# The residual stream of a two-layer trunk kept by rows between layers, with another order of the output projection and another split of the weight ring

## The chip, the core and the metric

One core of a Trainium2 chip. The metric is the device time of one execution of the whole kernel in microseconds, median of the runs. Its parts that matter here: TensorE (PE, matmuls and transposes through PSUM banks), VectorE (DVE), ScalarE (ACT), GpSimd (POOL), SyncE (SP, which issues all transfers). Each engine works through its own list of instructions in order and waits on semaphores.

## The reference, cut

Two layers over x of 512 rows (tokens) by 1024 columns, then a last norm, all in float32:

```
h = rmsnorm(x, norm_w)                  # rows of 1024
proj = h @ w_in                         # 1024 x 4160: 33 column tiles
y = concat(rwkv7(...), short_conv(...), moba_attention(...), retention(...)) * silu gates
x = x + y @ w_out                       # 1024 x 1024
...                                     # after both layers: out = rmsnorm(x, final_norm_w)
```

## The kernel before, in words

**Layout.** The stream x stands turned: `XY` holds 8 tiles of 128 model columns (partitions) by 512 tokens. The split copy of h, `act_hi` and `act_lo`, has the same layout. Every float32 product is made of three (high x high, low weight x high, high weight x low); `product(job, n)` issues the three for one of 8 blocks of the contraction, and a job is 8 such blocks, 24 matmuls of 512 columns (16 for `wa`).

**Norm.** At the start x is loaded by rows (4 tiles of 128 rows), turned by 32 transposes into `XY` and also spilled to scratch memory, since `XY` is used again for the gated outputs y. The sum of squares of the first layer is taken on the rows; rms is broadcast over the partitions by four small matmuls (`norm`), VectorE scales (`scaled`), ScalarE rounds to the high part, VectorE makes the low part (`low`), and TensorE starts the pair `k0`, `k1` tile by tile. Between layers the squares are added up by VectorE and summed over partitions by small matmuls (`stat`). After the last layer each output tile is turned back to rows by four transposes (`row`), multiplied by the final norm's weight, and at the very end scaled by 1/rms and stored.

**Weights.** The stream of a layer is 33 tiles of `w_in` (numbers 0 to 32: k0, k1, wa, r0, r1, v0, v1, rwkv_g0, rwkv_g1, rq0, rq1, rk0, rk1, rv0, rv1, ret_g0, ret_g1, mq0, mq1, mk0, mk1, mv0, mv1, moba_g0, moba_g1, cc0, ...) and 8 of `w_out`. SyncE loads tile i into one of `RAW` buffers when tile i - `RAW` is split. The high part goes to one of `HI` buffers when the job `HI` places earlier is through; it is made on ScalarE in `weight_high(job)`, called right behind each job's own evacuation, for tile number job + `HI`, or on GpSimd for the tiles in `POOL_HIGH`. GpSimd makes all low parts. ScalarE's list behind `weight_high` goes on with the evacuations of the next steps.

**Order.** `layer_steps()` writes one list of steps; each engine issues its part of every step in that order. Around tile 20 it reads: gate ret_g1; `to_rows("rk")` (8 transposes, two evacuations by ScalarE); `block_rows(2)` (VectorE, the end of the 16x16 block inverses); quarters 0 and 1 of mq0; `retain_state` on TensorE, which waits for those evacuations; and on. SyncE's list has, in front of the load of tile 18 (mq1), the copies of the score blocks out and back (`blocks_out`), and in front of the load of tile 20 (mk1):

```
def inverses_back(layer):
    sp.wait_ge(*at("blocks_done", layer))       # VectorE, block_rows(2)
    ...                                         # blocks out to scratch, then 8 loads back
if j == TILES.index("mk1"):
    inverses_back(layer)
load_weights(i)
```

**Output projection.** `project_out(m)`: eight jobs of 24 matmuls, weights stationary, y moving; the first two interleaved block by block as y gets split (`split_y`). VectorE adds each to the x tile that has come back from scratch (L1776).

Of the kernel before, what the change touches and what calls it, by code (L numbers as in the profile page):

```python
# [50 lines left out]
RAW, HI, LO = 3, 3, 3  # L51
# [18 lines left out]
OUT_TILES = [f"out{m}" for m in range(KT)]  # L70
STREAM = TILES + OUT_TILES

POOL_HIGH = ("mk1", "mv0", "mv1", "moba_g0")
# [11 lines left out]
MU, W0, A0, KKP, KAP, RKP, LNW, LNB, CONVW, NORMW = 0, 7, 9, 11, 13, 15, 17, 19, 21, 27  # L85
N_ROWS, N_PAR = 27, 35
# [6 lines left out]
CONSTS = [("ident", 128), ("eps", 2), ("one", 1), ("head_mean", 128), ("all_mean", 1), ("causal", 128),  # L93
# [44 lines left out]
def layer_steps():  # L138

    s = [("norm",), ("k_pair",)]  # L140
# [51 lines left out]
    s += [("conv_out", 1)] + [("split_y", k) for k in Y_ORDER[5:]] + [("project_out", m) for m in range(KT)]  # L192
# [15 lines left out]

Y_ORDER = [6, 7, 4, 5, 0, 1, 2, 3]
STEPS = layer_steps()  # L210


def bank_jobs():


    pro = [("norm_cols", 7, 1)] + [(f"x_in{m}", m, 1) for m in range(KT)] + [("params0", 3, 1), ("params1", 4, 1)]
# [3 lines left out]
    def proj(name, readers):  # L220
        if name not in projections:

            at = {"wa": 2, "out0": 0, "out1": 4}.get(name)
            if at is None:
                at = (int(name[3:]) + 1) % 2 if name.startswith("out") else (len(projections) - (len(projections) > 2)) % 2
            layer.append((name, at, readers))
            projections.append(name)
# [7 lines left out]
    for step in STEPS:  # L235
        kind = step[0]
        if kind == "norm":
            layer.append(("rn", 2, 0))
        elif kind == "k_pair":
# [55 lines left out]
        elif kind == "retain_values":  # L295
            layer.append((f"ret_y{step[1]}", 4, 1))
        elif kind == "retain_state":
            layer.append(("ret_state", 4, 1))
        elif kind == "ln_var":
            layer += [("var0", 7, 1), ("var1", 5, 1)]  # L300
        elif kind == "ret_stat":
            layer += [("ret_ms0", 2, 1), ("ret_ms1", 3, 1)]
        elif kind == "project_out":
            proj(f"out{step[1]}", 1)
            if step[1] == KT - 1:
                layer.append(("stat", 2, 1))
    epi = [(f"row{m}", 3 + m % 5, 1) for m in range(KT)]
    return pro, layer, epi


def trunk_kernel(nc, x, norm_w, w_in, w_out, rwkv_mu, rwkv_w0, rwkv_w2, rwkv_a0, rwkv_a2, rwkv_k_k,
                 rwkv_k_a, rwkv_r_k, rwkv_lnx_w, rwkv_lnx_b, conv_w, rel_bias, final_norm_w,
                 consts, level_masks, ret_eps, x_scratch, bias_scratch, a_scratch, t_scratch, tt_scratch, out):
    pro, per_layer, epi = bank_jobs()
    place = {}
    full_count, read_count = [0] * 8, [0] * 8
    for part, names in (("pro", pro), ("layer", per_layer), ("epi", epi)):
        if part == "layer":
            pro_full, pro_read = list(full_count), list(read_count)
            full_count, read_count = [0] * 8, [0] * 8  # L320
        if part == "epi":
            lay_full, lay_read = list(full_count), list(read_count)
            full_count, read_count = [0] * 8, [0] * 8
        for name, bank, readers in names:
            place[part, name] = (bank, full_count[bank], read_count[bank], readers)
            full_count[bank] += 1
            read_count[bank] += readers

    def locate(name, layer):


        part = "pro" if layer < 0 else "epi" if layer >= DEPTH else "layer"
# [6 lines left out]
    with ExitStack() as ctx:  # L339
# [16 lines left out]
        par = sb("params", [P, DEPTH, N_PAR])  # L356
        der = sb("params_derived", [P, DEPTH, N_DER])
        lora_w = sb("lora_w", [2 * LORA, DEPTH, G])
        small = sb("small", [P, 32])
# [19 lines left out]
        ident, head_mean, all_mean = const("ident"), const("head_mean"), const("all_mean")  # L379
# [19 lines left out]
        out_rows = pages[:, 17 * PG:(17 + NT) * PG].rearrange("p (t c) -> p t c", c=PG)  # L399
        norm_rows = page(10)[0:DEPTH * KT, 0:P]  # L400
# [6 lines left out]
        fnorm = page(2)  # L407
        row_sum, row_scale, row_max = small[:, 0:4], small[:, 4:8], small[:, 20:24]
        mean_sq, root, rms = small[:, 8:12], small[:, 12:16], small[:, 16:20]
        UW = pages[:, 21 * PG:21 * PG + 2048].rearrange("p (m x i) -> p m x i", m=MATS, x=2)  # L410
# [10 lines left out]
        def s(name):  # L421
# [9 lines left out]
            "h_raw": KT, "h_hi": KT, "h_split": KT,  # L431
# [29 lines left out]

        block = ctx.enter_context(nc.Block())
# [3 lines left out]
        def _(sp):  # L466
# [5 lines left out]
            load(norm_rows, norm_w.rearrange("l (k c) -> (l k) c", c=P), "norm_loaded")  # L472
# [3 lines left out]
            def load_weights(i):  # L476

                layer, j = divmod(i, n_stream)
                if i >= RAW:
                    sp.wait_ge(s("w_split"), i - RAW + 1)  # L480
                n = 2 * LORA if STREAM[j] == "wa" else P
                if j < len(TILES):
                    c = TILE_COLS[TILES[j]]
                    src = w_in[layer, :, c:c + n]
                else:
                    src = w_out[layer, :, (j - len(TILES)) * P:(j - len(TILES) + 1) * P]
                sp.dma_start(w_raw[:, i % RAW, :, 0:n], src.rearrange("(k p) c -> p k c", p=P)).then_inc(s(f"w_loaded{i % RAW}"), 16)
# [19 lines left out]
            load_weights(2)  # L507
# [45 lines left out]
            def spill_first_x():  # L553
                for m in range(KT):
                    sp.wait_ge(*read(f"x_in{m}", -1))
                    load(x_scratch[m], XY[:, m, :], "x_spill")

# [10 lines left out]
            i = RAW  # L568
            for layer in range(DEPTH):
                while i < (layer + 1) * n_stream:  # L570
                    j = i - layer * n_stream
                    if j == len(TILES) + 4:
                        if layer == DEPTH - 1:
                            sp.wait_ge(*full("moba_y1", layer))
                            load(fnorm, final_norm_w.rearrange("(r d) -> r d", r=1)[0].partition_broadcast(P), "fnorm_loaded")
                        for k, m in enumerate(Y_ORDER):
                            sp.wait_ge(*at("y_split", layer, k + 1))
                            sp.wait_ge(s("x_spill"), 16 * KT * (layer + 1))
                            load(XY[:, m, :], x_scratch[m], f"x_back{m}")
                    if i == 2 * RAW:  # L580
                        spill_first_x()
                    if i == 3 * RAW:
                        skew_bias()
                    if i == 4 * RAW:
# [12 lines left out]
                if layer < DEPTH - 1:  # L597
                    for k in range(RAW):
                        load_weights(i)
                        i += 1  # L600
                    for m in range(KT):
                        sp.wait_ge(*read(f"out{m}", layer))
                        load(x_scratch[m], XY[:, m, :], "x_spill")
# [3 lines left out]
            sp.wait_ge(s("stored"), 16 * NT)  # L607
# [3 lines left out]
        def _(pool):  # L611
# [5 lines left out]
            for i in range(DEPTH * n_stream):  # L617
                if i >= HI:
                    before = divmod(i - HI, n_stream)
                    pool.wait_ge(*full(STREAM[before[1]], before[0]))  # L620
                lora = STREAM[i % n_stream] == "wa"
                n = 2 * LORA if lora else P
                if high_on_pool(i):
                    pool.wait_ge(s(f"w_loaded{i % RAW}"), 16 * (i // RAW + 1))
                    for a in range(2):
                        k = slice(a * H, (a + 1) * H)
                        raw = w_raw[:, i % RAW, k, 0:n]
                        pool.tensor_tensor(w_hi[:, i % HI, k, 0:n], raw, const("one").unsqueeze(2).to_broadcast([P, H, n]), ALU.mult).then_inc(s("w_high_pool"), 1)  # L628
                for a in range(2):
                    k = slice(a * H, (a + 1) * H)  # L630
                    if high_on_pool(i):
                        pool.wait_ge(s("w_high_pool"), 2 * highs_before(i, True) + a + 1)
# [3 lines left out]
                    ins = pool.tensor_tensor(low, w_raw[:, i % RAW, k, 0:n], w_hi[:, i % HI, k, 0:n].bitcast(F32), ALU.subtract)  # L636
# [4 lines left out]
        def _(pe):  # L641
# [11 lines left out]

            pe.wait_ge(s("const_a"), 16)
            pe.wait_ge(s("norm_loaded"), 16)
            b = begin("norm_cols", -1)
# [1207 lines left out]
```

## Time and profile before

| | |
|---|---|
| median of 3 runs | 624.18 us (623.57 to 624.37) |
| the profiled execution | 624.2 us, of which span 622.4 us |
| TensorE busy | 596.7 us, 96% |
| VectorE, ScalarE, GpSimd busy | 61%, 42%, 40% |
| granted TensorE clock, mean | 0.995 |
| transfers | 66.26 MB, mean 106 GB/s |

The span runs from the first to the last instruction; the profiled execution's own time is 1.8 us longer. In the timelines, L1112 is line 1112 of the kernel before, "x8" is the number of instructions merged into a row, and the bracket at the end is the engine's idle time before the row and what ended it.

### The profile page before, as it was taken

The page shows a single profiled execution, that of the slowest core. Times are in us where ns is not written, and L with a number is a line of the kernel's source. Part 1 is how long each engine was busy: PE and PEld are TensorE (multiplying, and loading weights), DVE is VectorE, ACT ScalarE, POOL GpSimd, SP SyncE. Part 2 cuts the span into 40 slices and gives each one's busy share as a digit, 9 for nine tenths or more (in the row PEclk, how much of TensorE's full clock was granted, in tenths as well). Part 3 has the DMA queues.
Part 4 walks back from the last instruction along what each step waited for, and adds up shares of the span by engine and source line. Part 5 has one row for each costly group of instructions (what it writes and reads, how often), then busy time and mean ns, then how long its engine had stood idle before and what let it go on. Part 6 is the DMA issues. An engine that isn't in the chain of part 4 may idle for free.

```text
span 622.4 us, 11997 instructions
## 1 busy us (share of the span) xinstructions
PE 596.7 (96%) x4915; PEld 478.6 (77%) x4915; DVE 377.6 (61%) x642; ACT 263.9 (42%) x509; POOL 248.6 (40%) x192
## 2 busy tenths in 40 slices
PE   3999999999999999999989999999998999999994
PEld 3777878887877777878878787888786777787884
DVE  3858977471358457773275897746224846778433
ACT  4474432423155455533348443242314545644321
POOL 3564534413812223546506364431561313334720
PEclk9999999999999999999999999999999999999998
DMA  7948542526322121355443333252732212135403
GB/s 235 275 115 251 170 102 68 111 29 162 104 68 70 36 69 47 89 187 139 148 119 84 92 97 103 72 107 44 179 82 57 70 35 70 35 95 183 127 1 135
DMA packets 118711, 66.26 MB, mean 106 GB/s; under 512 B 29246, under 2 KB 111746, under 8 KB 118530
## 3 DMA queue, kind: packets, MB, share of 16 engines
q1 hardware_dynamic: 118658, 65.51, 38.5%
q8 instruction: 39, 0.64, 0.5%
q14 instruction: 14, 0.11, 0.1%
HBM read 55.26 MB, written 10.24 MB: 105 GB/s over the span
## 4 chain that ended last, share of the span: by engine, by line
PE 91%; DVE 3%; DMA 2%; issue 1%; ACT 1%; SPq 0%; POOL 0%; DVEq 0%; ACTq 0%; POOLq 0%
PE bank L704 25%; PE bank L707 23%; PE bank L706 23%; PE bank L808 2%; PE bank L878 2%; PE bank L905 2%; DMA pages<-in_x_dram 2%; PE bank L889 2%; PE bank L863 1%; PE bank L823 1%; PE bank L990 1%; PE bank L1025 1%; PE bank L837 1%; PE bank L1041 1%; PE bank L788 1%
## 5 line engine op out<-in xcount | busy, mean ns | idle before, releaser
L636 POOL TENSOR_TENSOR w_lo<-w_raw,w_hi 128x512 fp32r<-128x512 f32 x160 | 222.1, 1411 | 298.1 <-ACT w_hi L1112 298.1
L704 PE MATMUL bank<-act_hi,w_hi 128*128 128x512 f32 x656 | 264.5, 403 | 3.0 <-DVE act_lo L1765 1.3
L707 PE MATMUL bank<-act_lo,w_hi 128*128 128x512 f32 x656 | 256.0, 390 | 0.0
L706 PE MATMUL bank<-act_hi,w_lo 128*128 128x512 f32 x640 | 249.7, 390 | 0.0
L704 PEld LDWEIGHTS bank<-act_hi,w_hi 128*128 128x128 f32 x656 | 123.1, 188 | 40.6 <-issue 13.8
L707 PEld LDWEIGHTS bank<-act_lo,w_hi 128*128 128x128 f32 x656 | 123.1, 188 | 26.5
L706 PEld LDWEIGHTS bank<-act_hi,w_lo 128*128 128x128 f32 x640 | 120.3, 188 | 22.2
L1112 ACT ACTIVATE w_hi<-w_raw 128x512 fp32r<-128x512 f32 (+1 forms) x142 | 80.8, 619 | 52.6 <-PE bank L707 49.5
L1215 ACT ACTIVATE pages<-bank 128x512 f32<-128x512 f32 x24 | 14.3, 597 | 89.3 <-PE bank L707 89.3
L628 POOL TENSOR_TENSOR w_hi<-w_raw,constants 128x512 fp32r<-128x512 f32 (+1 forms) x22 | 22.5, 1042 | 48.2 <-DMA w_raw<-in_w_in_dram 44.6
L1776 DVE TENSOR_TENSOR x_or_y<-x_or_y,bank 128x512 f32<-128x512 f32 x16 | 11.0, 687 | 38.9 <-PE bank L707 38.9
L1248 ACT ACTIVATE pages<-pages,small 128x128 f32<-128x128 f32 (+3 forms) x32 | 17.9, 558 | 17.5 <-DVE small L1603 17.4
L1198 ACT ACTIVATE x_or_y<-bank 128x512 f32<-128x512 f32 x16 | 9.6, 598 | 36.3 <-PE bank L707 36.3
L1598 DVE SCALAR_TENSOR_TENSOR pages<-bank,bias 128x128 f32<-128x128 f32 (+3 forms) x32 | 14.8, 484 | 14.9 <-PE bank L878 14.7
L1533 DVE SCALAR_TENSOR_TENSOR x_or_y<-x_or_y,bank 128x512 f32<-128x512 f32 x16 | 10.9, 683 | 12.8 <-ACT x_or_y L1198 12.8
L1738 DVE RECIPROCAL pages<-pages 128x256 f32<-128x256 f32 x8 | 13.7, 1734 | 8.2 <-ACT pages L1330 8.2
L1254 ACT ACTIVATE pages<-bank 128x384 f32<-128x384 f32 (+1 forms) x24 | 11.4, 530 | 16.3 <-PE bank L889 16.3
L1773 DVE TENSOR_TENSOR pages<-pages 128x512 f32<-128x512 f32 x12 | 10.5, 877 | 12.8 <-ACT pages L1119 12.6
L1468 DVE TENSOR_TENSOR stat_lo<-pages,stat_hi 128x512 fp32r<-128x512 f32 x16 | 15.4, 981 | 3.8 <-ACT pages L1162 3.6
L1153 ACT ACTIVATE pages<-bank,params_derived 128x512 f32<-128x512 f32 x12 | 8.2, 687 | 21.5 <-PE bank L707 20.8
L1566 DVE COPY_PREDICATED pages<-level_mask,bank 128x512 f32<-128x512 uint8 x4 | 2.7, 733 | 23.2 <-PE bank L850 23.2
L1572 DVE COPY_PREDICATED pages<-level_mask,bank 128x512 f32<-128x512 uint8 x8 | 5.5, 735 | 17.6 <-PE bank L863 17.6
(188 smaller groups left out, 749.5 us busy)
## 6 DMA issues: line engine op xcount, KB each, us to landing
w_raw<-in_w_in_dram SPq DMA_DIRECT2D x64, 512.0 KB, 4.1
w_raw<-in_w_out_dram SPq DMA_DIRECT2D x16, 512.0 KB, 3.8
x_scratch<-x_or_y SPq DMA_DIRECT2D x16, 256.0 KB, 4.1
x_or_y<-x_scratch SPq DMA_DIRECT2D x16, 256.0 KB, 2.8
pages<-in_x_dram SPq DMA_DIRECT2D x4, 512.0 KB, 9.0
out_dram<-pages SPq DMA_DIRECT2D x4, 512.0 KB, 3.9
bias_scratch<-pages SPq DMA_DIRECT2D x1, 1280.0 KB, 7.4
constants<-in_consts_dram SPq DMA_DIRECT2D x1, 1064.5 KB, 5.8
```

Source lines behind the costliest of these rows:

```text
L628: pool.tensor_tensor(w_hi[:, i % HI, k, 0:n], raw, const("one").unsqueeze(2).to_broadcast([P, H, n]), ALU.mult).then_inc(s("w_high_pool"), 1)
L636: ins = pool.tensor_tensor(low, w_raw[:, i % RAW, k, 0:n], w_hi[:, i % HI, k, 0:n].bitcast(F32), ALU.subtract)
L704: mm(b[:, :], hi, act_hi[:, k, :], start=n == 0, stop=False)
L706: mm(b[:, :], lo, act_hi[:, k, :], start=False, stop=False)
L707: ins = mm(b[:, :], hi, act_lo[:, k, :], start=False, stop=n == KT - 1)
L808: ins = pe.transpose(b[:, t * P:(t + 1) * P], src[:, p, t * P:(t + 1) * P], ident)
L1112: go(w_hi[:, i % HI, k, 0:n], w_raw[:, i % RAW, k, 0:n], ACT.Copy).then_inc(s("w_high"), 1)
L1215: go(dst, ps(job, layer)[:, :], ACT.Copy).then_inc(done(job, layer), 1)
L1248: go(pb, pb, ACT.Exp, bias=row_max[:, n:n + 1], accum_out=row_sum[:, n:n + 1]).then_inc(s("prob"), 1)
L1468: tt(stat_lo[:, p, :], square[:, p, :], stat_hi[:, p, :].bitcast(F32), ALU.subtract).then_inc(s(f"{what}_split"), 1)
L1598: ins = stt(PB[:, hh, c0:c0 + w], ps(job, layer)[:, c0:c0 + w], 0.125, bias[:, 2 * p + hh, T - w:T], ALU.mult, ALU.add)
L1738: mark(dve.reciprocal(v, v))
```

## The change

The stream is kept by rows. Output products are made with y stationary (128 tokens) and `w_out` moving (512 model columns), so PSUM holds rows: four row tiles by two halves of 512 columns, eight banks. Each weight tile of `w_out` is now 2 contraction blocks by 512 columns. The first half's sums (`o0_t`) are finished after slot 3 and their squares taken; slots 5 to 7 are gone through per row tile (`out_end`), so the row tiles finish one after another. `row_norm(t)` takes the squares along the free axis, root and reciprocal, multiplies with the next norm's weight, and only the normed rows are turned (`turn`, 8 transposes per row tile). In the last layer the normed rows are stored from where they stand, in halves. The pair k0, k1 runs in two halves of 256 tokens, with the last two turns in between. x is not spilled at the start (it is read again from the input), x tiles 0 and 1 are loaded ahead of the weights of k0 and k1, and these two tiles are loaded as one pair in two pieces. Of the two `row_norm(t)` in the diff the first is ScalarE's, the second VectorE's. The weight ring is 2 raw, 4 high and 4 low buffers instead of 3, 3, 3, and `POOL_HIGH` names mv0, mv1, moba_g0, moba_g1.

```diff
-RAW, HI, LO = 3, 3, 3
+RAW, HI, LO = 2, 4, 4
...
-POOL_HIGH = ("mk1", "mv0", "mv1", "moba_g0")
+OUT_SLOTS = [f"out{q}" for q in range(8)]
+OUT_EARLY = (0, 1, 2, 4, 5, 6)
+POOL_HIGH = ("mv0", "mv1", "moba_g0", "moba_g1")
...
-    s = [("norm",), ("k_pair",)]
+    s = [("k_pair",)]
...
-    s += [("conv_out", 1)] + [("split_y", k) for k in Y_ORDER[5:]] + [("project_out", m) for m in range(KT)]
+    s += [("conv_out", 1)] + [("split_y", k) for k in Y_ORDER[5:]] + [("out", q) for q in range(5)] + [("out_end",)]
...
+        def raw_in(i, a):
+            if i < 2:
+                return s(f"first_loaded{a}"), 16
+            return s(f"w_loaded{i % RAW}"), 16 * (i // RAW)
...
             load_x(0)
-            load(bias_table, rel_bias.partition_broadcast(P), "bias_in")
-            load_weights(0)
             load_x(1)
+            load_first_pair(0)
+            load_first_pair(1)
             load_x(2)
             load_x(3)
-            load_weights(1)
...
-                    if i == 2 * RAW:
-                        spill_first_x()
...
+            b = begin("k0", 0)
+            for _ in range(14):
+                mm(b[:, 0:P], ident, ident, start=True, stop=True)
...
+                def k_part(job, first, ns):
+                    cols = slice(first * P, (first + 2) * P)
+                    for n in ns:
...
+                        mm(b[:, cols], hi, act_hi[:, n, cols], start=n == 0, stop=False)
+                        mm(b[:, cols], lo, act_hi[:, n, cols], start=False, stop=False)
+                        ins = mm(b[:, cols], hi, act_lo[:, n, cols], start=False, stop=n == KT - 1)
...
+                def k_pair():
+                    k_part("k0", 0, range(0, 4))
+                    turn(2, layer)
+                    k_part("k0", 0, range(4, 8))
+                    k_part("k1", 0, range(0, 1))
+                    turn(3, layer)
+                    k_part("k1", 0, range(1, 8))
+                    if layer == 0:
+                        params()
+                    k_part("k0", 2, range(8))
+                    k_part("k1", 2, range(8))
...
+                def out_rows(q, ts):
...
+                            mm(b[:, :], act_hi[:, k, tc], hi[:, wc], start=first, stop=False)
+                            mm(b[:, :], act_hi[:, k, tc], lo[:, wc], start=False, stop=False)
+                            ins = mm(b[:, :], act_lo[:, k, tc], hi[:, wc], start=False, stop=last)
...
+                def out_end():
+                    for t in (0, 1):
+                        for q in (5, 6, 7):
+                            out_rows(q, [t])
+                    if layer < DEPTH - 1:
+                        turn(0, layer + 1)
+                    out_rows(5, [2, 3]).then_inc(s("out_used"), 1)
+                    out_rows(6, [2])
+                    if layer < DEPTH - 1:
+                        turn(1, layer + 1)
+                    out_rows(7, [2])
+                    out_rows(6, [3]).then_inc(s("out_used"), 1)
+                    out_rows(7, [3])
...
             def weight_high(job, layer):
                 i = layer * len(STREAM) + STREAM.index(job) + HI
                 if i >= DEPTH * len(STREAM) or high_on_pool(i):
                     return
-                act.wait_ge(*full(job, layer))
-                act.wait_ge(s(f"w_loaded{i % RAW}"), 16 * (i // RAW + 1))
+                act.wait_ge(*used(job, layer))
+                act.wait_ge(*raw_in(i, 0))
...
+                def row_norm(t):
+                    act.wait_ge(*read(f"o1_{t}", layer))
+                    go(half(23 + t // 2, t % 2), XY[:, 2 * t + 1, :], ACT.Square, scale=D ** -0.5, accum_out=mean_sq[:, t:t + 1]).then_inc(s("sq_last"), 1)
...
+                    go(root[:, t:t + 1], mean_sq[:, t:t + 1], ACT.Sqrt, bias=sq_base[:, t:t + 1]).then_inc(s("root"), 1)
...
+                    go(h_rows(t, 0), h_rows(t, 0), ACT.Copy, scale=rms[:, t:t + 1]).then_inc(s("h_rows0"), 1)
...
+                def row_norm(t):
+                    invert_root(t, layer + 1)
+                    dve.wait_ge(*read(f"o1_{t}", layer))
+                    stt(h_rows(t, 1), XY[:, 2 * t + 1, :], rms[:, t:t + 1], norm_next[:, T:2 * T], ALU.mult, ALU.mult).then_inc(s("h_rows1"), 1)
...
             for t in range(NT):
-                sp.wait_ge(s(f"scaled{t}"), 1)
-                sp.dma_start(out[0, t * P:(t + 1) * P, :], page(17 + t)).then_inc(s("stored"), 16)
+                for a in range(2):
+                    sp.wait_ge(*at(f"h_rows{a}", DEPTH, t + 1))
+                    sp.dma_start(out[0, t * P:(t + 1) * P, a * T:(a + 1) * T], h_rows(t, a)).then_inc(s("stored"), 16)
```

## Rows read from the trace of the kernel before

**Rows 1.** The page: busy time of each engine; the chain that ended last.

```profile
PE 596.7 (96%) x4915; PEld 478.6 (77%) x4915; DVE 377.6 (61%) x642; ACT 263.9 (42%) x509; POOL 248.6 (40%) x192
...
PE 91%; DVE 3%; DMA 2%; issue 1%; ACT 1%; SPq 0%; POOL 0%; DVEq 0%; ACTq 0%; POOLq 0%
```

**Rows 2.** Timeline of SyncE, layer 0 (start us, us, engine, line, what).

```profile
133.98 0.37 SPq L468 DMA_DIRECT2D t_scratch<-pages  x1
...
140.10 2.67 SPq L468 DMA_DIRECT2D pages<-tt_scratch  x4
142.82 21.56 SPq L487 DMA_DIRECT2D w_raw<-in_w_in_dram  x6
```

**Rows 3.** Timeline of GpSimd, layer 0.

```profile
149.62 2.04 POOL L628 TENSOR_TENSOR w_hi<-w_raw,constants 128x512 fp32r<-128x512 f32 x2 [18.30 <-DMA w_raw<-in_w_in_dram]
```

**Rows 4.** Timeline of ScalarE behind job ret_g1, layer 0.

```profile
127.84 1.14 ACT L1112 ACTIVATE w_hi<-w_raw 128x512 fp32r<-128x512 f32 x2
128.88 1.07 ACT L1231 ACTIVATE pages<-bank 128x512 f32<-128x512 f32 x2
```

**Rows 5.** Timeline of TensorE, layer 0: retain_state.

```profile
130.84 1.08 PE L1014 MATMUL bank<-pages 128*64 128x64 f32 x24
```

**Rows 6.** Timeline of GpSimd, layer 1.

```profile
442.91 2.04 POOL L628 TENSOR_TENSOR w_hi<-w_raw,constants 128x512 fp32r<-128x512 f32 x2 [16.77 <-DMA w_raw<-in_w_in_dram]
```

**Rows 7.** Timeline of TensorE, layer 1: retain_state.

```profile
425.67 1.08 PE L1014 MATMUL bank<-pages 128*64 128x64 f32 x24
```

**Rows 8.** Busy time by stretch, the end (engines, granted clock, transfers' share, GB/s).

```profile
618.00:620.00 2.00, 0.00 (x0) 0.00 (x0) 0.00 (x0) 0.00 (x0) 0.00 (x0) 0.50 1.02 412
```

**Rows 9.** Transposes by line: ns min/median/max of one, first and last start.

```profile
L662 PE MATMUL bank<-constants,pages x32: 273/418/475, 5.6 to 16.2; 128*128 128x128 f32 x32
...
L686 PE MATMUL bank<-constants,x_or_y x32: 270/273/330, 575.9 to 613.1; 128*128 128x128 f32 x32
```

**Rows 10.** Timeline of TensorE, start of the kernel.

```profile
11.74 4.70 PE L662 MATMUL bank<-constants,pages 128*128 128x128 f32 x24 [4.15 <-DMA pages<-in_x_dram]
...
18.75 2.05 PE L728 MATMUL bank<-constants 128*128 128x128 f32 x16
21.14 0.47 PE L704 MATMUL bank<-act_hi,w_hi 128*128 128x512 f32 x1 [0.34 <-DVE act_lo L1409]
```

**Rows 11.** Timeline of ScalarE, start of the kernel.

```profile
5.61 1.06 ACT L1095 ACTIVATE pages<-pages 128x1024 f32<-128x1024 f32 x1 [2.15 <-DMA pages<-in_x_dram]
```

**Rows 12.** Timeline of GpSimd, start of the kernel.

```profile
10.59 2.05 POOL L628 TENSOR_TENSOR w_hi<-w_raw,constants 128x512 fp32r<-128x512 f32 x2 [8.65 <-DMA w_raw<-in_w_in_dram]
12.59 2.51 POOL L636 TENSOR_TENSOR w_lo<-w_raw,w_hi 128x512 fp32r<-128x512 f32 x2
```

**Rows 13.** Timeline of TensorE, first product of r0 in layer 0.

```profile
37.13 0.50 PE L704 MATMUL bank<-act_hi,w_hi 128*128 128x512 f32 x1 [0.56 <-POOL w_lo L636]
```

**Rows 14.** Timeline of TensorE, output projection of layer 0 to the next layer.

```profile
267.14 0.47 PE L704 MATMUL bank<-act_hi,w_hi 128*128 128x512 f32 x1 [0.67 <-DVE act_lo L1765]
...
310.53 0.39 PE L707 MATMUL bank<-act_lo,w_hi 128*128 128x512 f32 x1
310.75 0.95 PE L676 MATMUL bank<-constants,pages 128*128 128x1 f32 x8
...
317.45 0.47 PE L704 MATMUL bank<-act_hi,w_hi 128*128 128x512 f32 x1 [0.53 <-DVE act_lo L1409]
```

**Rows 15.** Timeline of VectorE, the end of the kernel.

```profile
611.65 0.69 DVE L1776 TENSOR_TENSOR x_or_y<-x_or_y,bank 128x512 f32<-128x512 f32 x1 [3.86 <-PE bank L707]
```

**Rows 16.** Timeline of ScalarE, the end of the kernel.

```profile
612.38 0.63 ACT L1119 ACTIVATE pages<-x_or_y 128x512 f32<-128x512 f32 x1 [5.30 <-DVE x_or_y L1776]
614.16 0.26 ACT L1124 ACTIVATE small<-bank,constants 128x4 f32<-128x4 f32 x1 [1.15 <-PE bank L676]
```

**Rows 17.** Timeline of SyncE, the end of the kernel.

```profile
615.52 2.87 SPq L606 DMA_DIRECT2D out_dram<-pages  x4
```

**Rows 18.** The stores of the output: us from issue to landing.

```profile
DMA to landing us min/median/max: 2.7/3.9/4.7
```

More of the change, by code:

```diff
@@ L302, in bank_jobs @@
             layer += [("ret_ms0", 2, 1), ("ret_ms1", 3, 1)]
[L303 to L308, printed above, removed]
+        elif kind == "out":
+            if step[1] % 4 == 0:
+                layer += [(f"o{step[1] // 4}_{t}", t if step[1] else 4 + t, 1) for t in range(NT)]
+        elif kind == "out_end":
+            layer += turns
+    return pro, layer
 def trunk_kernel(nc, x, norm_w, w_in, w_out, rwkv_mu, rwkv_w0, rwkv_w2, rwkv_a0, rwkv_a2, rwkv_k_k,
@@ L651, in end, with turn @@
                 ins.then_inc(bank_full[locate(job, layer)[0]], 1)
+            def turn(t, layer):
+                for a in range(2):
+                    pe.wait_ge(*at(f"h_rows{a}", layer, t + 1))
+                    b = begin(f"h{t}{a}", layer - 1)
+                    for j in range(NT):
+                        ins = pe.transpose(b[:, j * P:(j + 1) * P], h_rows(t, a)[:, j * P:(j + 1) * P], ident)
+                    end(ins, f"h{t}{a}", layer - 1)
             pe.wait_ge(s("const_a"), 16)
@@ L666, in stat @@
-            def stat(layer, last):
-                b = ps("stat", layer) if last else begin("stat", layer)
-                if last:
-                    pe.wait_ge(s("x_sq"), (layer + 1) * KT)
-                else:
-                    pe.wait_ge(s("sq_added"), (layer + 1) * (KT - 2))
-                src = half(24, 1) if last else half(11, 0)
-                for t in range(NT):
-                    ins = mm(b[:, t:t + 1], src[:, t * P:(t + 1) * P], const("all_mean"),
-                             start=not last and t == 0, stop=last, skip_group_check=True)
-                if last:
-                    end(ins, "stat", layer)
@@ L681, in row @@
-            def row(m):
-                pe.wait_ge(*read(f"out{m}", DEPTH - 1))
-                b = begin(f"row{m}", DEPTH)
-                for t in range(NT):
-                    ins = pe.transpose(b[:, t * P:(t + 1) * P], XY[:, m, t * P:(t + 1) * P], ident)
-                end(ins, f"row{m}", DEPTH)
+            for a in range(2):
+                b = begin(f"nw{a}", -1)
+                end(mm(b[:, :], const("one")[0:1, :].to_broadcast([1, P]), norm_row[:, a * T:(a + 1) * T], start=True, stop=True), f"nw{a}", -1)
@@ L1444, in pads @@
+            dve.tensor_copy(mean_r[:, :], head_mean).then_inc(s("mean_r"), 1)
+            for layer in range(DEPTH):
                 def pads():
@@ L1781, in _, with add_out, out @@
-                run = dict(norm=norm, shift=shift, kk_input=lambda: stat_low("kk", KN), ret_low=lambda: stat_low("ret", RSQ),
+                def add_out(a, t):
+                    dve.wait_ge(*full(f"o{a}_{t}", layer))
+                    dve.wait_ge(s(f"x_back{t}"), 16 * (layer + 1))
+                    tt(XY[:, 2 * t + a, :], XY[:, 2 * t + a, :], ps(f"o{a}_{t}", layer)[:, :], ALU.add).then_inc(done(f"o{a}_{t}", layer), 1)
+                def out(q):
+                    if q != 3:
+                        return
+                    for t in ROW_ORDER:
+                        add_out(0, t)
+                    dve.wait_ge(s("next_loaded"), 16 * (layer + 1))
+                    for t in ROW_ORDER:
+                        dve.wait_ge(*read(f"o0_{t}", layer))
+                        tt(h_rows(t, 0), XY[:, 2 * t, :], norm_next[:, 0:T], ALU.mult).then_inc(s("h_weighted"), 1)
+                    dve.wait_ge(*at("sq_first", layer))
+                    ts(sq_base, first_sq, NORM_EPS, None, ALU.add).then_inc(s("sq_base"), 1)
```

417 lines of the change are left out of this document (203 added, 214 removed).

## The prediction

> **What bounds the kernel now.** I read the page first: TensorE is busy 96% of the span and makes up 91% of the chain that ended last [rows 1]. So an instruction taken from TensorE is time saved, one added is time lost, and work on the other engines costs nothing until TensorE waits for it. Then I read the timelines at the places the diff touches, to see where TensorE waits now (start, boundary of the layers, end) and where it could begin to wait: where SyncE, ScalarE and GpSimd stand when the weight ring changes from 3 raw + 3 split to 2 raw + 4 split. That last look decides this prediction.
>
> **Part 1: ScalarE comes to wait for a late weight tile.** `weight_high(job)` runs on ScalarE behind each job and makes the high part of the tile `HI` places further on. Tile `mk1` is number 20 of the stream. SyncE issues its load only after `inverses_back`, and that waits for VectorE's block inverses: in layer 0 the scratch copy goes out at 133.98, the reads back follow until 142.8, and only then comes the load of `mk1`, at 142.82 [rows 2]. GpSimd, which makes both parts of `mk1` in the kernel before (it is in `POOL_HIGH`), gets the data at 149.62 after idling 18.30 us [rows 3]. Nobody suffers: ScalarE is not involved, and job `ret_g1` (number 16) makes tile 19 at 127.84 [rows 4].
>
> With `HI` = 4, job 16 makes tile 20, and the diff takes `mk1` out of `POOL_HIGH`. So ScalarE, at 127.84, waits for a transfer that lands at 149.62. Nothing in the diff lets it land sooner: the load still stands behind `inverses_back` (those lines are not in the diff), that depends on VectorE's `block_rows(2)`, which needs nothing of ScalarE after the tanh of `ret_g1`, and on SyncE's own copies. So it is a stall, not a deadlock, and its end stays where it is.
>
> Queued behind the waiting instruction are the two evacuations of `rows_rk` [rows 4]. `retain_state` on TensorE waits for them; it starts at 130.84 now [rows 5]. TensorE has only the transposes and the first half of `mq0` in front of it, and those are already before 130.84. In the kernel after, the evacuations end at 149.62 + 1.14 (the two high copies) + 1.07 = 151.83, so TensorE stands still for 151.83 - 130.84 = **21.0 us** in layer 0. In layer 1 the tile lands at 442.91 [rows 6] and `retain_state` now starts at 425.67 [rows 7]: 442.91 + 2.21 - 425.67 = **19.4 us**. TensorE being the bound, nothing gives this back: the waits it would have had later are near zero.
>
> After such a pause TensorE may restart slowly. The granted clock reads 1.00 while it works and 0.50 (1.2 GHz of 2.4) some microseconds after its last instruction [rows 8]; at the kernel's start a transpose takes 418 ns at the median against 273 ns later [rows 9]. The 24 transposes of the start take 4.70 us [rows 10] where at 0.11 each they would take 2.6: 2.1 lost, part of it to the arrivals of x among them. I cost one restart at 1.7 us, twice **3.4**; ends 0 (no fall) and 4.6.
>
> The same shift puts tile 18 (`mq1`, loaded behind the score blocks' copies) on ScalarE at job `rv1`, some 4 us before it has landed. Behind it stand evacuations whose banks TensorE wants 6 us later, so I cost this at nothing; if that cover were gone it would be 1 us a layer.
>
> **Part 2: the start.** x tile 0 lands at 5.61 [rows 11] as before, tile 1 no longer stands behind a weight tile and a broadcast. Square 1.06, sum read-out, root and reciprocal 0.7, two products with the norm row 1.4: the first normed row tile is ready near 8.7, the second near 10.3. Sixteen transposes at 0.23 (the rate of the start) end near 12.0. Then 14 keep-warm matmuls: 16 records (8 matmuls) take 2.05 [rows 10], so 14 take 3.6, and some of them at the slow level make it 4.2: the first product of `k0` at 16.2. Its weights, 4.6 us of GpSimd work per tile [rows 12] behind a transfer landing near 8.5 and 10, are ready near 13 and 17.7, in time. Before, that product stood at 21.14: -4.9. From there to the first product of `r0` at 37.13 [rows 13] are 64 matmuls of 0.227, 14.5 us, so 1.5 us of stalls go too. Sixteen transposes (turns 2 and 3) come in, 16 x 0.11 = +1.8, and the params transposes, +0.3. Together **-4.3** (ends 0, if the keep-warms all run slowly and a row tile is late, and -5.5).
>
> **Part 3: the boundary.** The 192 matmuls of the output projection stay 192 of 512 columns; from 267.14 to 310.53 there are 191 steps of 0.2272 [rows 14]. The hole behind them, 310.75 to 317.45 (sums of squares, root, broadcast of rms, keep-warm, first split), is 6.7 us and goes. 32 transposes come in, 3.5 us. What hides the row norms is the next tile's matmuls: add 0.69, square 0.8, root 0.3, reciprocal 0.2, product 0.7 and hops make 3.1 us, against 4.1 us (18 matmuls) for tiles 0 and 1 and about 4 us for 2 and 3 (`k0` and `k1` halves); slack about 1 us, so I add nothing. **-3.2**, upper end -1. Last, tiles 6 and 7 of `w_out` come from a raw ring of two behind the return of x; I have them split some 2 us before use.
>
> The `k0`/`k1` pair now runs in halves: 96 matmuls of 256 columns a layer for 48 of 512. No row shows 256 columns. From below: half of 0.2272, 0.114. From above: on the line between 0.11 for a transpose of 128 columns and 0.227 for 512, 0.149. The keep-warm records, each with a weight load of its own, follow each other in 0.118 [rows 10]; I take 0.122, near them. 192 x 0.122 = 23.4 against 96 x 0.2272 = 21.8: **+1.6** (ends +0.1 and +6.8). The Trainium skill ("TensorE: Matmul & The Clock Gate", Part 3, What overlaps and what doesn't) says that a weight load overlaps running matmuls only when the row groups differ, and they do not here; by that it would stand open before every matmul.
>
> **Part 4: the end.** The 28 row transposes between output tiles go (28 x 0.11 = 3.1), so the last output matmul ends near 608.5. Behind it now: add at 611.65 [rows 15], square at 612.38, root at 614.16 [rows 16], three scalings, and 2 MB of stores, first issued at 615.52 [rows 17], landing 2.7 to 4.7 us after issue [rows 18]. After: three of the four row tiles are stored by then. For the last: add 0.69, square 0.8, root 0.26, reciprocal 0.18, product 0.69, hops 0.3: 611.4. Two stores of 256 KB, 0.4 more for the second issue, 2.8 to land, 0.5 to close: 615.1 against 622.4, **-7.3** (ends -6 and -8.2).
>
> **Sum.** 21.0 + 19.4 + 3.4 - 4.3 - 3.2 + 1.6 - 7.3 = +30.6. The profiled execution took 624.2 (span 622.4 and 1.8 around it), as the median of the runs, 624.18. So **654.8**.
>
> **Rivals.** (a) *The other side: no stall.* If ScalarE did not wait for `mk1`, because its transfer were issued before the block inverses are done, or if TensorE needed nothing of ScalarE meanwhile, only the savings would stand: 624.2 - 4.3 - 3.2 - 7.3 + 1.6 = 611.0. It turns at the landing: `mk1` would have to be there by 127.84 + about 15 for the stall to be no more than the 13 that is saved. For it: GpSimd now idles 18 us for the same tile and costs nothing. Against: that is because GpSimd has nothing queued that TensorE wants, and ScalarE has. 8%. (b) *The weight load stands open before 256 columns.* Eight loads with one column each take 0.95 us [rows 14], 0.10 apart; 0.114 + 0.10 = 0.212, x192 = 40.7, +17.3 on my sum: 672. This is the skill's rule above at work. Against: at 512 columns it would make 0.31 of what the trace shows as 0.227 [rows 14], so the trace does not agree with the rule. 3%. (c) *The change's savings fail but the stall comes*: row norms late at the boundary, slow keep-warms: 654.8 + 6 = 661. In the range. (d) *A stall somewhere else too*, with a ring of two raw tiles landing at one per 4 us: 665 or more. 3%.
>
> **How the numbers follow.** The forecast with (c) has 86%. Its range: low end without slow restarts (-3.4), with the best ends of parts 2 and 4 (-2.1), the lowest 256-column price (-1.5) and some 2 us for a tile that lands sooner, 646; high end with most of the savings of parts 2 and 3 failed or the upper 256-column price, and restarts at 4.6, 664; all of these together are less likely than the 14% outside. That leaves out (a), (b) and (d), 14%. A measurement of this kernel can tell about 0.2% from no change. Faster is (a) and a little, 0.09; same 0.01; slower 0.90.
>
> **What would show it.** ScalarE's high copies behind `ret_g1` idle some 21 us, released by the transfer of w_raw, once a layer; TensorE idle at `retain_state` some 20 us, released by ScalarE, and nothing else above 2 us there; granted clock below 1.00 in and after those holes. First `k0` product near 16, `r0` near 34; no hole between output projection and `k0` of layer 1; 256-column matmuls 0.12 apart; the last store about 6.5 us behind the last matmul. Wrong would be: `retain_state` without a wait, or ScalarE's wait ending long before the inverses are back.

## The result, and the profile after

The kernel after takes **647.86 us** (646.78 to 648.92, 4 runs) against 623.88 (623.03 to 624.37, 4 runs) of the kernel before: 1.0386 times as long, 95% interval 1.0364 to 1.0408. The forecast was 654.8, in a range of 646 to 664. The profiled execution took 648.3, its span 646.3.

The page first: busy time, TensorE in 40 slices, the granted clock in the same slices, and the chain that ended last, which answer to [rows 1].

```profile
PE 597.9 (93%) x4962; PEld 482.2 (75%) x4962; DVE 369.7 (57%) x634; ACT 268.7 (42%) x534; POOL 246.8 (38%) x194
...
PE   7999999809999999999999999992699999999996
...
PEclk9999999958999999999999999998699999999999
...
PE 73%; DMA 1%; issue 1%; SPq 1%; DVE 1%; ACT 1%; ACTq 0%; DVEq 0%
```

TensorE works as long as before; what is lost are two holes, each with a dip of the clock, and after the savings elsewhere 24 us of them are left. The waits of TensorE name them (total, times, longest):

```profile
PE bank L1033 <- ACT pages L1262: 34.3, 2, 17.3
PE bank L692 <- DMA constants<-in_consts_dram: 2.8, 1, 2.8
PE bank L685 <- DVE pages L1454: 1.6, 1, 1.6
...
PE bank L989 <- issue: 1.2, 1, 1.2
PE bank L908 <- issue: 0.6, 1, 0.6
```

L1033 is `retain_state`, L1262 the evacuations of `rows_rk`. The hole of layer 0 in ScalarE's, SyncE's and TensorE's timelines (answering to [rows 2, 4, 5]):

```profile
123.32 0.60 ACT L1229 ACTIVATE x_or_y<-bank 128x512 f32<-128x512 f32 x1 [2.86 <-PE bank L714]
141.85 1.15 ACT L1168 ACTIVATE w_hi<-w_raw 128x512 fp32r<-128x512 f32 x2 [17.94 <-DMA w_raw<-in_w_in_dram]
142.91 1.06 ACT L1262 ACTIVATE pages<-bank 128x512 f32<-128x512 f32 x2
```

```profile
128.19 0.37 SPq L489 DMA_DIRECT2D t_scratch<-pages  x1
...
136.66 8.86 SPq L512 DMA_DIRECT2D w_raw<-in_w_in_dram  x3
```

```profile
144.23 1.79 PE L1033 MATMUL bank<-pages 128*64 128x64 f32 x24 [17.34 <-ACT pages L1262]
145.95 2.08 PE L1044 MATMUL bank<-pages 64*128 64x128 f32 x16
```

Read upwards: `retain_state` waits for ScalarE, ScalarE for the tile, and the tile's load stands behind the copies of the inverses. In layer 1 the same three stand at 458.10, 455.73 and 450.87. Behind the hole the instructions are slow at first: 1.79 us for the 24 small matmuls that took 1.08 before [rows 5], and 2.08 for the 16 behind them that took 1.16. Windows (engines' busy time, granted clock, transfers' share, GB/s):

```profile
127.00:131.00 4.00, 0.00 (x0) 0.00 (x0) 1.47 (x4) 0.00 (x0) 0.00 (x0) 1.00 0.43 51
...
135.00:139.00 4.00, 0.00 (x0) 0.00 (x0) 0.00 (x0) 0.00 (x0) 0.00 (x0) 0.50 0.91 181
...
146.00:148.00 2.00, 2.00 (x18) 1.78 (x17) 0.58 (x2) 0.49 (x1) 0.00 (x0) 0.50 0.82 205
...
150.00:152.00 2.00, 2.00 (x10) 1.65 (x9) 1.70 (x2) 0.41 (x1) 0.36 (x1) 1.00 0.00 0
```

Where the time went, by marks in TensorE's timeline (first start of each):

| stretch | before | after | difference |
|---|---|---|---|
| start to r0, layer 0 | 37.13 | 32.52 | -4.6 |
| r0 to transposes of rk | 90.0 | 90.6 | +0.6 |
| to retain_state | 3.7 | 21.1 | **+17.4** |
| to the output projection | 136.3 | 140.6 | +4.3 |
| to r0 of layer 1 (the boundary) | 65.0 | 62.4 | -2.6 |
| r0 to transposes of rk | 89.9 | 90.2 | +0.3 |
| to retain_state | 3.7 | 20.8 | **+17.1** |
| to the output projection | 139.0 | 138.5 | -0.5 |
| output projection | 46.6 | 43.4 | -3.2 |
| last matmul to the end | 11.2 | 6.3 | -4.9 |

The sum is +23.9. In the two stretches behind the holes, the slow restart is 2.2 and 2.3 (the shift of the same instruction grows from 13.4 to 15.6, and from 32.4 to 34.7). The rest, +2.1 and -2.7, are for the most part waits called "issue" (idle time for which the profile shows no cause): 1.7 and 0.5 us of them stood in layer 1 before, 1.2 and 0.6 stand in layer 0 after.

The start, the boundary and the end, in TensorE's timeline, then VectorE's at the end (answering to [rows 10, 14, 15]):

```profile
11.57 3.80 PE L697 MATMUL bank<-constants 128*128 128x128 f32 x28
15.13 0.36 PE L750 MATMUL bank<-act_hi,w_hi 128*128 128x256 f32 x1
15.33 0.28 PE L751 MATMUL bank<-act_hi,w_lo 128*128 128x256 f32 x1
15.45 0.28 PE L752 MATMUL bank<-act_lo,w_hi 128*128 128x256 f32 x1
...
330.05 0.39 PE L1096 MATMUL bank<-w_hi,act_lo 128*128 128x512 f32 x1
330.27 0.28 PE L750 MATMUL bank<-act_hi,w_hi 128*128 128x256 f32 x1
```

```profile
640.41 0.69 DVE L1799 TENSOR_TENSOR x_or_y<-x_or_y,bank 128x512 f32<-128x512 f32 x1
642.22 0.16 DVE L1436 RECIPROCAL small<-small 128x1 f32<-128x1 f32 x1 [1.12 <-ACT small L1389]
642.42 0.75 DVE L1816 SCALAR_TENSOR_TENSOR pages<-x_or_y,small,pages 128x512 f32<-128x512 f32 x1
```

At the boundary k0 of layer 1 follows the last output matmul (330.05) in one step of the pitch. At the end the add starts 0.4 behind the last matmul (639.99), and the rows are scaled 3.2 behind it.

### The profile page after: what moved, and what is told of

The parts are those of the page before. It is cut to its first block, busy times and chain, and to the rows that moved or that the text cites. A ratio compares the mean times of both kernels' runs of the same rounds, so it can differ in the third digit from the quotient of the medians.

```text
span 646.3 us, 12071 instructions
## 1 busy us (share of the span) xinstructions
PE 597.9 (93%) x4962; PEld 482.2 (75%) x4962; DVE 369.7 (57%) x634; ACT 268.7 (42%) x534; POOL 246.8 (38%) x194
## 4 chain that ended last, share of the span: by engine, by line
PE 73%; DMA 1%; issue 1%; SPq 1%; DVE 1%; ACT 1%; ACTq 0%; DVEq 0%
PE bank L711 15%; PE bank L714 13%; PE bank L713 13%; PE bank L1094 5%; PE bank L1095 4%; PE bank L1096 4%; PE bank L897 2%; PE bank L924 2%; PE bank L908 2%; PE bank L882 1%; PE bank L827 1%; PE bank L1044 1%; SPq L489 1%; DMA w_raw<-in_w_in_dram 1%; PE bank L1009 1%
## 5 line engine op out<-in xcount | busy, mean ns | idle before, releaser
L711 PE MATMUL bank<-act_hi,w_hi 128*128 128x512 f32 x496 | 201.7, 407 | 0.4 <-DVE pages L1489 0.4
L714 PE MATMUL bank<-act_lo,w_hi 128*128 128x512 f32 x496 | 194.0, 391 | 0.0
L713 PE MATMUL bank<-act_hi,w_lo 128*128 128x512 f32 x480 | 187.9, 391 | 0.0
L1168 ACT ACTIVATE w_hi<-w_raw 128x512 fp32r<-128x512 f32 x140 | 79.7, 621 | 93.6 <-DMA w_raw<-in_w_in_dram 51.8
L711 PEld LDWEIGHTS bank<-act_hi,w_hi 128*128 128x128 f32 x496 | 93.5, 188 | 30.6 <-issue 11.7
L714 PEld LDWEIGHTS bank<-act_lo,w_hi 128*128 128x128 f32 x496 | 93.4, 188 | 20.1
L713 PEld LDWEIGHTS bank<-act_hi,w_lo 128*128 128x128 f32 x480 | 90.6, 189 | 16.5
L1094 PE MATMUL bank<-w_hi,act_hi 128*128 128x512 f32 x128 | 50.2, 392 | 1.3 <-issue 1.3
L1096 PE MATMUL bank<-w_hi,act_lo 128*128 128x512 f32 x128 | 49.9, 390 | 0.0
L1095 PE MATMUL bank<-w_lo,act_hi 128*128 128x512 f32 x128 | 49.8, 389 | 0.0
L656 POOL TENSOR_TENSOR w_hi<-w_raw,constants 128x512 fp32r<-128x512 f32 (+1 forms) x20 | 21.1, 1056 | 41.6 <-PE bank L714 41.6
L1033 PE MATMUL bank<-pages 128*64 128x64 f32 x48 | 3.6, 317 | 34.3 <-ACT pages L1262 34.3
L1033 PEld LDWEIGHTS bank<-pages 128*64 128x64 f32 x48 | 3.3, 222 | 35.1 <-issue 35.1
```

The source lines that it names most:

```text
L711: mm(b[:, :], hi, act_hi[:, k, :], start=n == 0, stop=False)
L713: mm(b[:, :], lo, act_hi[:, k, :], start=False, stop=False)
L714: ins = mm(b[:, :], hi, act_lo[:, k, :], start=False, stop=n == KT - 1)
L1094: mm(b[:, :], act_hi[:, k, tc], hi[:, wc], start=first, stop=False)
L1095: mm(b[:, :], act_hi[:, k, tc], lo[:, wc], start=False, stop=False)
L1096: ins = mm(b[:, :], act_lo[:, k, tc], hi[:, wc], start=False, stop=last)
```

## The experiments

### Is it mk1 on ScalarE, or its place behind the inverses?

Two edits of the kernel after, each alone.

```diff
-POOL_HIGH = ("mv0", "mv1", "moba_g0", "moba_g1")
+POOL_HIGH = ("mk1", "mv0", "mv1", "moba_g0", "moba_g1")
```

> The kernel after with mk1 added to POOL_HIGH (five tiles on GpSimd), nothing else. Theory (the whole loss is ScalarE standing behind the transfer of mk1): retain_state waits for nothing, the two stalls of 17.3 and 17.0 us and the two slow restarts (2.2 each, read from the shift of the products behind retain_state) go, 647.9 - 34.3 - 4.4 = 609.1 us; granted clock about 0.99. Rival 1 (the transfer stall hid another one, from two raw buffers or from GpSimd's load of five tiles of 4.6 us): 614 or more, with a new wait of TensorE above 2 us behind tile 20. Rival 2 (the stall is not ScalarE's but comes with the score blocks themselves): no change, 648.

```diff
-if j == TILES.index("mk1"):
+if j == TILES.index("mv0"):
     inverses_back(layer)
```

> The kernel after with inverses_back placed behind the load of mk1 instead of in front of it (ahead of mv0), POOL_HIGH as in the kernel after, so ScalarE still makes mk1. Theory (it is the place of the transfer in SyncE's list that makes ScalarE wait): the tile lands near 120, ScalarE does not wait at ret_g1, 609 us as with mk1 on GpSimd, within 1. Rival (the high copies of mk1 on ScalarE themselves are in the way of TensorE, or the copies back come too late behind the load): 612 or more.

Measured: **608.18** (0.9747 of before, 0.9729 to 0.9765) and **608.31** (0.9748, 0.9731 to 0.9765). In the second, the load of mk1 follows those of mq1 and mk0, and ScalarE passes ret_g1 without a wait (SyncE's timeline, then ScalarE's):

```profile
108.99 9.22 SPq L512 DMA_DIRECT2D w_raw<-in_w_in_dram  x3
129.70 0.37 SPq L489 DMA_DIRECT2D t_scratch<-pages  x1
```

```profile
123.56 1.14 ACT L1168 ACTIVATE w_hi<-w_raw 128x512 fp32r<-128x512 f32 x2
```

Both remedies give the same time, so the cause is the pair: who makes the tile, and where its load stands. Once the constants have arrived, TensorE then waits nowhere more than 1.7 us, so two raw buffers and five tiles on GpSimd hide no second stall here. The 39.7 us that come back are the holes, 34.5, and the restarts, 4.5, within 0.7.

### The harm alone, in the order of the kernel before

```diff
-RAW, HI, LO = 3, 3, 3
+RAW, HI, LO = 2, 4, 4
-POOL_HIGH = ("mk1", "mv0", "mv1", "moba_g0")
+POOL_HIGH = ("mv0", "mv1", "moba_g0", "moba_g1")
```

> The kernel before with only the ring (2 raw, 4 high, 4 low) and the new POOL_HIGH, the start and the boundary of the layers unchanged. Theory: the harm alone, both stalls as in the kernel after: 623.9 + 34.3 + 4.4 = 662.6 us. The stall is 17.3 and not the 21.0 forecast because tile 19 is split on GpSimd one job earlier, no longer beside VectorE's last block products: those take 0.40 and 0.47 us here too, against 1.51 and 1.10 before. Rival (the stall is shorter because of the new start or stream): 21.0 + 19.4 + 4.4, 668.7 us.

With the second line of that edit alone:

> The kernel before with the new POOL_HIGH alone, the ring still 3, 3, 3. ScalarE then makes mk1 one job later, behind mq0 (about 136.6 in layer 0), and waits until it lands at 149.6. Queued behind are not the rows of rk but the evacuations of retention's output and of the chunk inverses; TensorE wants the latter near 147 in layer 0 and 442 in layer 1, and they come some 6.2 and 4.7 us late: 624 + 11 = 635 us. Rival (any wait of ScalarE for mk1 costs as much as in the kernel after): 660. Rival (all hidden): 624.

With the first line, and mk1 beside the four new names:

> The kernel before with the ring 2, 4, 4 and five tiles on GpSimd, mk1 among them. Theory: both stalls at retain_state go, and what stays of the ring's price in the old order is the wait of 6.4 us at the boundary (ScalarE makes the high part of r0 of the next layer ahead of the last squares, and that tile is loaded behind the eight spills of x), with its slow restart: 624 + 6.4 + 1.5 = 632. Rival (the 9 us that the ring cost beyond the two stalls are spread over many tiles, from two raw buffers): about 632 too, but with waits of TensorE at many lines and none of 6 us at L676.

Measured: **671.88** (1.0773, 1.0747 to 1.0799), **637.38** (1.0217, 1.0199 to 1.0235), **632.58** (1.0144, 1.0130 to 1.0158). The waits of TensorE in the first of them:

```profile
PE bank L1014 <- ACT pages L1231: 34.0, 2, 17.1
PE bank L676 <- ACT pages L1119: 6.4, 1, 6.4
```

The holes have the length of those in the kernel after, not the 21.0 and 19.4 of the forecast, so the new start and the new stream have no part in it. Of the missing 9 us (6.7 in the profiled execution, which took 669.3), 6.4 were a wait that I had not foreseen: with four high buffers ScalarE makes r0 of the next layer before the last squares, and in the old order its load stands behind eight spills of x. It is the same fault at another place. The third run has it, 6.5 us at L676, and the two holes are gone. Its profiled span is 9.4 us longer than before: 7.5 at the boundary up to r0, the wait and a slow restart with the granted clock at 0.50 from 316 to 324; and 1.7 in layer 0, two waits of 0.7 and 0.9 before 60 us that the theory did not have. So the 632.6 near the forecast of 632 is in part luck. In its ScalarE's timeline:

```profile
318.11 1.15 ACT L1112 ACTIVATE w_hi<-w_raw 128x512 fp32r<-128x512 f32 x2 [9.59 <-DMA w_raw<-in_w_in_dram]
319.17 0.61 ACT L1119 ACTIVATE pages<-x_or_y 128x512 f32<-128x512 f32 x1
```

In the second run (ring of three) ScalarE waits 11.1 us for mk1 behind mq0. By then its rows of rk are out, and TensorE wants only the chunk inverses, 4.2 and 4.4 us late (ScalarE's, then TensorE's timeline):

```profile
147.64 1.15 ACT L1112 ACTIVATE w_hi<-w_raw 128x512 fp32r<-128x512 f32 x2 [11.12 <-DMA w_raw<-in_w_in_dram]
...
150.13 1.09 ACT L1276 ACTIVATE pages<-bank 128x512 f32<-128x512 f32 x2
```

```profile
151.37 1.98 PE L837 MATMUL bank<-pages 64*64 64x64 f32 x64 [4.22 <-ACT pages L1276]
```

TensorE is slow behind this short wait too: the granted clock reads 0.50 from 152 to 156, and the shift against the kernel before grows from 4.2 to 6.9 us in layer 0 and by 1.5 in layer 1. So a short wait can carry as dear a restart as a long one.
A wait of ScalarE of 11 us a layer costs 13.4 for both layers (8.6 of it waits of TensorE, 4.2 slow restarts), one of 18 us 39: what counts is what is queued behind it.

### The restart

Filling matmuls ahead of `retain_state` in the kernel after, first 140 and then 70 a layer; the output is unchanged, they write a bank that is overwritten.

```diff
+b = begin("ret_state", layer)
+for _ in range(140):                       # 70 in the second
+    mm(b[:, 0:P], ident, ident, start=True, stop=True)
 for q in range(2):
     pe.wait_ge(*read(f"rows_rv{q}", layer))
```

> The kernel after (647.9 us), its stall left as it is, with 140 matmuls of 128 columns (ident by ident) ahead of retain_state in each layer, in the time in which TensorE stands. Theory (the shift of 2.2 us behind each stall is the clock, 1.2 GHz after the idle time): TensorE starts retain_state at the same moment, at the fast level, and 4.4 us come back: 643.5. Rival (the first products behind the stall are slow for another reason, as weights or transfers): 647.9.

> As the filled stall before, with 70 filling matmuls and not 140: in the trace of that run 280 records took 31.43 us, 0.224 a matmul doubled to two records, so 140 took longer than the stall. 70 take 15.7 us and end 1.7 before retain_state can start. Theory: the stall ends where it did, retain_state and the products behind it run at the fast level, 647.9 - 4.4 = 643.5 us. Rival (the filling matmuls delay something, or the slow restart comes back after the 1.7 us of idle time): 646 to 648.

The first missed: **671.36** (1.0761, 1.0746 to 1.0775). Each float32 matmul is two records of 0.112, so 140 filled 31.4 us and ran past the stall. The second gave **644.90** (1.0349, 1.0331 to 1.0367), 3.0 less than the kernel after. Its TensorE:

```profile
125.51 15.79 PE L1028 MATMUL bank<-constants 128*128 128x128 f32 x140
142.30 1.05 PE L1035 MATMUL bank<-pages 128*64 128x64 f32 x24 [0.99 <-ACT pages L1264]
```

The 24 matmuls take 1.05 and not 1.79, those behind them are at the fast pitch at once, and the granted clock reads 1.00 from 142 to 146 us, where the kernel after has 0.50 from 144 to 148:

```profile
142.00:144.00 2.00, 1.70 (x36) 1.67 (x38) 0.04 (x1) 0.64 (x2) 1.30 (x2) 1.00 0.01 2
```

So the restart is the clock. The idle 1.0 and 1.7 us that were left brought no slow restart. From the start of `retain_state` to the fourth product of 512 columns behind it pass 2.87 us in both layers, against 5.08 and 5.15 in the kernel after: 4.5 us are back. The span is only 3.5 shorter: the "issue" waits of this kernel are 1.9 longer, and the start up to the transposes of rk is 1.2 shorter.

### The row tiles one after another, and the halves

From here on the base is the first experiment's kernel, 608.18 us.

```diff
-for t in (0, 1):
-    for q in (5, 6, 7):
-        out_rows(q, [t])
...
+for q in (5, 6, 7):
+    out_rows(q, range(NT))
```

> The first run's kernel (608.2 us) with the output slots 5, 6 and 7 taken one after another for all four row tiles, turns 0 and 1 behind them. All row tiles then finish within the last 12 matmuls (2.7 us). VectorE's list takes add, wait for the root, scaling, tile by tile, 3.1 us each: the last rows are ready 10.6 us behind the last matmul and not 3.1 (+7.5 at the end), and at the boundary k0 waits for the low part of row tile 1, some 6.5 us. Sum 622. Rival (row tile by row tile buys nothing, the chain of norms is short enough): 610.

Measured **621.55** (0.9969, 0.9958 to 0.9980). VectorE at the end goes through add, wait, scaling four times:

```profile
607.48 0.69 DVE L1793 TENSOR_TENSOR x_or_y<-x_or_y,bank 128x512 f32<-128x512 f32 x1 [12.15 <-PE bank L1096]
...
617.27 0.16 DVE L1430 RECIPROCAL small<-small 128x1 f32<-128x1 f32 x1 [1.11 <-ACT small L1383]
617.47 0.75 DVE L1810 SCALAR_TENSOR_TENSOR pages<-x_or_y,small,pages 128x512 f32<-128x512 f32 x1
```

The last matmul starts at 609.09 and the span ends 12.3 later against 6.4: 5.9 of the 15.0 us in the span, where I had 7.5. At the boundary (output projection to r0 of layer 1) 7.6 are lost, with a slow restart in them, where I had 6.5. The other 1.4 are at the start and in layer 0, where the edit changes nothing (0.8 of them: from the first of the 14 keep-warms to the first product it took 4.0 us here and 3.2 in the base). So 621.55 meets the forecast of 622 partly by luck. The order by row tiles is worth 13.4 of the 15.8 us that the change gains with mk1 on GpSimd.

```diff
-k_part("k0", 0, range(0, 4)); turn(2, layer); k_part("k0", 0, range(4, 8)); ...
+turn(2, layer); turn(3, layer); k_part("k0", 0, range(8)); k_part("k1", 0, range(8))   # 512 columns
```

> The first run's kernel (608.2 us) with k0 and k1 in whole 512 columns, all four turns ahead of them. Theory (the halves hide the norms of row tiles 2 and 3): the start has to wait for the low part of row tile 3, near 19.9, so r0 comes 2.1 later; at the boundary k0 waits some 6 us behind the last output matmul for norm, turn and split of row tile 3, less 0.6 for the pitch (96 products of 0.120 against 48 of 0.227): +4.5. Sum 615. Rival (the next matmuls hid them anyway): 607.

Measured **612.94** (0.9827, 0.9811 to 0.9842). r0 comes 0.8 later, not 2.1 (k0 starts at 18.38, not 19.9). At the boundary:

```profile
311.84 1.09 PE L685 MATMUL bank<-constants,pages 128*128 128x128 f32 x8 [1.64 <-ACT pages L1388]
314.34 0.54 PE L750 MATMUL bank<-act_hi,w_hi 128*128 128x512 f32 x1 [1.41 <-DVE act_lo L1440]
```

k0 follows the last output matmul (308.58) after 5.8, and from the output projection to r0 it takes 4.9 us longer than in the base, forecast 4.5. The halves hide that, as forecast.

### The keep-warms

0 and 5 of them for 14, on the same base.

> The first run's kernel (mk1 on GpSimd, 608.2 us) without the 14 keep-warm matmuls at the start. There they stand between the turns (end 11.6) and the first product of k0 (14.95), but GpSimd has split k0 only at 13.2 and k1 at 17.9, so 1.7 us of them is exposed, of which the split of k1 gives back all but 0.7. Theory (they buy the fast clock): without them the products of k0 run some microseconds at 1.2 GHz, 1 to 3 us more than is gained: 609 to 611. Rival (the turns alone have raised the clock): 607.5. Both are small: the trace decides by the pitch of the first 256-column products, 0.12 or about 0.22.

> The kernel of the first run with 5 keep-warms and not 14 or 0. Without any, TensorE stood 1.4 us for the split of k0, then ran its first 12 products 0.215 apart and not 0.120, and the time was 606.55 against 608.18 with 14. Five take 1.2 us, fill that wait and no more. Theory: the first product at 12.9, the fast level sooner by the time filled: 605.5 to 606.5. Rival (the gain of the run without any was the change in its issue stalls, 0.3 to 0.5 us of waits against 1.6 before, and not the start): 607 to 608.

Measured **606.55** (0.9723, 0.9710 to 0.9736) with none and **606.73** (0.9719, 0.9706 to 0.9733) with five; the intervals with 14 just overlap. TensorE, without and with five:

```profile
12.88 0.58 PE L747 MATMUL bank<-act_hi,w_hi 128*128 128x256 f32 x1 [1.38 <-POOL w_lo L661]
13.25 0.42 PE L748 MATMUL bank<-act_hi,w_lo 128*128 128x256 f32 x1
13.47 0.42 PE L749 MATMUL bank<-act_lo,w_hi 128*128 128x256 f32 x1
```

```profile
13.11 0.39 PE L750 MATMUL bank<-act_hi,w_hi 128*128 128x256 f32 x1 [0.68 <-POOL w_lo L661]
...
17.83 0.38 PE L750 MATMUL bank<-act_hi,w_hi 128*128 128x256 f32 x1 [0.71 <-POOL w_lo L661]
```

Without any, 12 products stand 0.215 apart; five keep them at 0.120. With five, TensorE waits 0.7 us for GpSimd's split of k0 and 0.7 for that of k1: there GpSimd bounds the start, not the clock. Against 14 keep-warms, r0 comes 0.3 earlier with none and 0.7 with five. So my theory of a loss fell: the slow products (12 at 0.095 more, and a slow turn, 1.5 us in all) cost less than the 1.9 us by which the first product comes sooner (12.88 for 14.80; the 14.95 of my expectation was misread). The rest of the 1.5 us goes with shorter "issue" waits, which no edit here controlled. The 606.73 with five lies between my two forecasts, so the times decide nothing between 0 and 5, and little between these and 14.

## Why the prediction came true, by its steps

**Part 1.** Mechanism, place and both layers as forecast; the first two experiments show the cause, the filled stall the restart. The sizes of the stall were off: 17.4 and 17.1 for 21.0 and 19.4. The step that failed is "its end stays where it is": I took the times of before for the landing. VectorE's last block products ended sooner. Their two rows before, with GpSimd's split of tile 19 beside them, and after:

```profile
128.60 2.71 POOL L636 TENSOR_TENSOR w_lo<-w_raw,w_hi 128x512 fp32r<-128x512 f32 x2 [4.55 <-ACT w_hi L1112]
```

```profile
128.65 1.51 DVE L1554 TENSOR_TENSOR pages<-pages 128x144 f32<-128x144 f32 x1
...
130.53 1.10 DVE L1554 TENSOR_TENSOR pages<-pages 128x169 f32<-128x169 f32 x1
```

```profile
124.63 0.40 DVE L1583 TENSOR_TENSOR pages<-pages 128x144 f32<-128x144 f32 x1
...
125.40 0.47 DVE L1583 TENSOR_TENSOR pages<-pages 128x169 f32<-128x169 f32 x1
```

With `HI` = 4 the split stands one job earlier (118.74) and no longer beside them: 1.7 us. Both kernels with the ring of three show 1.51, and ten of the eleven with the ring of four 0.40. The eleventh tells that it is GpSimd and not the ring: with the load of mk1 first, ScalarE makes mk1 at once, GpSimd's split of it falls beside the same two products, and they are slow again (GpSimd's, then VectorE's timeline):

```profile
124.32 2.72 POOL L661 TENSOR_TENSOR w_lo<-w_raw,w_hi 128x512 fp32r<-128x512 f32 x2 [2.89 <-ACT w_hi L1168]
```

```profile
124.37 1.52 DVE L1583 TENSOR_TENSOR pages<-pages 128x144 f32<-128x144 f32 x1
...
126.26 1.11 DVE L1583 TENSOR_TENSOR pages<-pages 128x169 f32<-128x169 f32 x1
```

The Trainium skill ("GPSIMD Engine Reference", section 1, Specifications) says that GpSimd contends with VectorE's instructions of two SBUF inputs. The trace agrees, and the reduction between the two products, with one input, kept its 0.30 beside the split. The rest is the transfer itself, 5.2 and 4.9 us from issue for 6.8 and 5.6 (and 0.4 of the copies in layer 0); it varied from 4.6 to 6.8 between kernels, and what sets it stays open. Restarts: 4.5 for 3.4. The late tile 18 cost nothing, as said (ScalarE waits 5.0 and 5.6 us for it, TensorE for nobody).

**Part 2.** The first k0 product at 15.1, forecast 16.2; r0 at 32.5. With its share of the 256-column price I had -3.5; measured -4.6. The row tiles were turned 0.4 sooner and the keep-warms took 3.6.

**Part 3.** No hole and no norm on the path: -2.6 for -2.4 with the price of the halves. The pitch of 256 columns is 0.120, forecast 0.122. Rival (b) is dead. The Trainium skill's rule ("TensorE: Matmul & The Clock Gate", Part 3, What overlaps and what doesn't), by which each of these products would show its weight load, does not hold in this trace.

**Part 4.** -3.2 and -4.9, together -8.1 for -7.3. The stores of 256 KB landed 2.2 us after issue at the median, where I had 2.8.

**Sum.** Stalls 5.9 less than forecast, restarts 1.1 more, savings some 2 more: 647.9 for 654.8. Rival (a), 611.0 without the stall, is the kernel of the first experiment: 608.2.

## What to carry to other kernels

When a ring gets deeper, list for every tile which engine makes it and at which job, and compare with the issue of its load and with what that load stands behind. An in-order engine that makes weights between evacuations turns a late tile into a late evacuation; move either the tile to an engine with nothing urgent queued, or its load ahead of the wait. A large rewrite can be right in each part and lose to one name in a list: here the rewrite saves 2.5% once mk1 is dealt with.

## What the runs showed of the hardware

- A VectorE product of two SBUF operands (128x144) took 1.51 us beside a GpSimd subtraction and 0.40 alone, so moving GpSimd's work shifts VectorE's chain.
- At the start without keep-warms the products of 256 columns stand 0.215 apart and not 0.120, while the granted clock's row reads 1.00 (12 to 16 us); after the holes, where the small matmuls are slow too, it reads 0.50. At the start, the pitch tells the level and that row does not.
- TensorE's slow restart cost 2.2 to 2.3 us behind holes of 17 us and 2.7 and 1.5 behind waits of 4.2 and 4.4; behind 1.0 and 1.7 us of idle time there was none.
- "Issue" waits of 0.2 to 1.5 us move between lines and layers from kernel to kernel, and their sum ran from 1.3 (without any keep-warms, and with five) to 5.0 us (the shorter filling). What causes them was not tried; they blur differences of up to 0.6%.
